# Sums across partitions: 56 small products a layer replaced by 32x32 turns and row sums, and one modulation group moved

## The chip, the core and the metric

The kernel runs on one core of one Trainium2 chip. The metric is the device time of one execution, in microseconds. Its engines work side by side and wait for each other through semaphores: TensorE (matrix products), VectorE (DVE), ScalarE (ACT), GpSimd (POOL), and SyncE (SP), whose queue here issues nearly all DMAs. An instruction is issued only when those before it in its own engine's program have been issued, so a wait holds everything behind it.

## The reference

Two layers of a decoder trunk, 1024 tokens of width 1024, all in f32. What matters here is the first half of a layer:

```python
mod = c_act @ ada_w[l] + ada_b[l]                      # six groups of 1024
sh1, sc1, g1, sh2, sc2, g2 = split(mod, 6)
h = rmsnorm(x, norm1_g[l]) * (1.0 + sc1) + sh1
proj = h @ w_in[l]                                     # in-projection, 20 column groups
y_ssd = ssd_mixer(...)                                 # conv, dt, chunked scan over 8 chunks of 128
y_mla = mla_mixer(...)                                 # rmsnorm(cq) @ w_uq, rmsnorm(ckv) @ w_ukv, attention
y_swa = swa_sink_mixer(...)
x = x + g1 * (concat(y_ssd, y_mla, y_swa) @ w_out[l])
h = rmsnorm(x, norm2_g[l]) * (1.0 + sc2) + sh2         # then the gated channel mixer, g2
```

Two kinds of sums across the partitions are touched: the sums over c of `c_act @ ada_w` for the groups g1, sh2, sc2, g2, and, per token, the sums of squares of the latents cq (256 channels) and ckv (128) for their RMS norms.

## The kernel before

A layer starts with the in-projection. The activations h lie with channels on partitions; the weight matrix is taken in 20 **packs** of 128 columns (pack 0: dt and the rotary key; 1 and 2: cq; 3: ckv; 4 to 11: the convolved channels; 12 to 15: the gate z; 16 to 19: the sliding-window heads). For each pack SyncE loads 512 KB into one of two `raw` tiles, ScalarE rounds it to a hi half (L984), GpSimd takes the lo half (L982), and TensorE does eight **K steps** of six 128x128x512 products (L1062): hi by hi, hi by lo, lo by hi, for two halves of the tokens. A pack's result stays in a bank pair (pack number mod 2) until ScalarE has copied it out, or, for packs 4 to 11, until VectorE has added three shifted taps of the convolution (L2216). Pack m waits for the release of pack m-2's bank (`pair_free`).

Between K steps TensorE is given other work by `scan_after`. In pack 7: the sums of squares of the latents. ScalarE has squared cq and ckv (L1774); `latent_sums` takes each 128x128 block as the stationary operand and one column of ones as the moving one, three products for each of eight blocks (L1143, L1144). In packs 10 and 11: the modulation sums. VectorE has multiplied 128 rows of `ada_w` at a time by `c_act` and added them up into an accumulator of 128x1024 for each of four groups (`early_products`, L2178 and L2181); `ada_half` sums its partitions with eight products of one column each (L1131). From pack 12 on: the **scan**, one chunk of 128 tokens in each pack's time. Its chain for chunk ch: ScalarE makes the decays from a tile that SyncE spreads over all partitions (`load_spread`, `cumSpread`, L790; `decays`, L1761 to L1766), VectorE multiplies the off-chunk part (`chunk_off`, L2287) and masks the scores (`mix`, L2252, L2254), TensorE does the diagonal products (`scan_back`, L1209).

The order on each engine is that of its program, written by hand. On VectorE: `early_products(0)` (eight passes), `dt_work` (a chain of passes of 8x1024 whose middle waits for ScalarE's Ln, and whose first part, `dt_sum`, that Ln waits for), then for j = 0 to 7 the taps of pack 4+j and, behind them, what the loop over j lists; then the scan. On ScalarE pack 1's eviction stands behind that Ln, and `decays(ch+1)` stands ahead of the hi half of pack 14+ch and of the eviction of pack 12+ch. On SyncE: ahead of pack 18's load stand eight loads of the latent up-projections (`wuq`, `wukv`), which go into the places of two modulation accumulators and so wait for `ada_part`; behind pack 18's load stands `load_spread(4)`, the fifth spread of decays.

Tiles share places. The weights `adaE` of groups 1 to 3 lie where x has been stored away; nt[2] and nt[3] are the accumulators of groups 0 and 1, and groups 2 and 3 accumulate in their own first tile. In layer 0 GpSimd also computes, in attention, the first two modulation groups of layer 1 (`ada_products`).

## Time and profile before

| | |
|---|---|
| median of 3 runs | 2359.29 us (2356.12 to 2361.5) |
| span of the profiled execution | 2356.7 us |
| TensorE busy | 2288.9 us, 97% of the span, 11493 products |
| VectorE busy | 1630.9 us, 69% |
| ScalarE, GpSimd busy | 1100.2 us, 1009.3 us |
| DMA | 310.98 MB, mean 132 GB/s |

The page gives the profiled execution's time by its span alone; the median of the runs is 2.6 us above it. "Busy" counts the time in which an engine works; TensorE's products are pipelined, so a group of rows can overlap the next by a few hundred ns. A wait in brackets behind a row is the idle time ahead of it and what ended it. The granted clock is TensorE's, 1.00 being the 2.4 GHz level and 0.50 the 1.2 GHz level.

### The profile page before, as it was taken

The page shows a single profiled execution, that of the slowest core. Times are in us where ns is not written, and L with a number is a line of the kernel's source. Part 1 is how long each engine was busy: PE and PEld are TensorE (multiplying, and loading weights), DVE is VectorE, ACT ScalarE, POOL GpSimd, SP SyncE. Part 2 cuts the span into 40 slices and gives each one's busy share as a digit, 9 for nine tenths or more (in the row PEclk, how much of TensorE's full clock was granted, in tenths as well). Part 3 has the DMA queues.
Part 4 walks back from the last instruction along what each step waited for, and adds up shares of the span by engine and source line. Part 5 has one row for each costly group of instructions (what it writes and reads, how often), then busy time and mean ns, then how long its engine had stood idle before and what let it go on. Part 6 is the DMA issues. An engine that isn't in the chain of part 4 may idle for free.

```text
span 2356.7 us, 31193 instructions
## 1 busy us (share of the span) xinstructions
PE 2288.9 (97%) x11493; PEld 1858.7 (79%) x11493; DVE 1630.9 (69%) x2084; ACT 1100.2 (47%) x1808; POOL 1009.3 (43%) x641
## 2 busy tenths in 40 slices
PE   5999999999899999999999999999999999999998
PEld 5788866788788888888878888668878888888887
DVE  6975457538876766777898644773697667677886
ACT  4335546524444444444452455673444444445455
POOL 1211268534987777400002123242479777760000
PEclk7999999999999999999999999999999999999999
DMA  8651323242333333487555331004414333347763
GB/s 287 221 196 54 77 63 117 99 139 85 92 112 90 112 90 117 144 293 252 156 194 191 108 85 55 10 20 153 142 41 125 112 90 112 90 130 254 246 214 112
DMA packets 272630, 310.98 MB, mean 132 GB/s; under 512 B 36905, under 2 KB 191263, under 8 KB 271455
## 3 DMA queue, kind: packets, MB, share of 16 engines
q1 hardware_dynamic: 272094, 307.94, 40.5%
q8 instruction: 92, 1.51, 0.3%
q10 hardware_dynamic: 384, 1.05, 0.2%
q14 instruction: 60, 0.48, 0.1%
HBM read 246.47 MB, written 61.42 MB: 131 GB/s over the span
## 4 chain that ended last, share of the span: by engine, by line
PE 80%; DVE 11%; ACT 2%; issue 2%; POOL 1%; DMA 1%; DVEq 0%; SPq 0%; ACTq 0%; POOLq 0%
PE bank L1489 30%; PE bank L1504 17%; PE bank L1062 16%; PE bank L1122 5%; DVE nt L2181 2%; PE bank L1320 2%; PE bank L1352 1%; PE bank L1280 1%; DVE hLo L2135 1%; PE bank L1380 1%; DVE xT L2129 1%; DMA raw<-in_ffn_w_up_dram 1%; PE bank L1209 1%; PE bank L1131 1%; DVE nt L2113 1%
## 5 line engine op out<-in xcount | busy, mean ns | idle before, releaser
L982 POOL TENSOR_TENSOR wLo<-raw,wHi 128x1024 fp32r<-128x1024 f32 x66 | 162.9, 2469 | 438.2 <-ACT wHi L984 438.2
L1681 POOL TENSOR_TENSOR prodLo<-comb,prodHi 128x512 fp32r<-128x512 f32 x160 | 234.3, 1471 | 123.6 <-ACT prodHi L1024 123.6
L1489 PE MATMUL bank<-tHi,prodHi 128*128 128x512 f32 x640 | 250.5, 391 | 5.2 <-DVE tLo L2493 4.1
L1489 PE MATMUL bank<-tLo,prodHi 128*128 128x512 f32 x640 | 249.9, 390 | 0.0
L1489 PE MATMUL bank<-tHi,prodLo 128*128 128x512 f32 x640 | 249.8, 390 | 0.0
L1504 PE MATMUL bank<-gateHi,downHi 128*128 128x512 f32 x616 | 240.5, 390 | 0.0
L1504 PE MATMUL bank<-gateHi,downLo 128*128 128x512 f32 x616 | 239.9, 389 | 0.0
L1504 PE MATMUL bank<-gateLo,downHi 128*128 128x512 f32 x616 | 239.8, 389 | 0.0
L1024 ACT ACTIVATE prodHi<-comb 128x512 fp32r<-128x512 f32 x160 | 100.5, 632 | 249.4 <-PE bank L1489 229.6
L2438 DVE SCALAR_TENSOR_TENSOR ub<-bank,ffp,ub 128x1023 f32<-128x1023 f32 x88 | 112.8, 1282 | 141.8 <-ACT ub L1943 140.2
L1062 PE MATMUL bank<-hHi,wHi 128*128 128x512 f32 x576 | 188.1, 408 | 5.4 <-ACT cq L1813 4.4
L1489 PE MATMUL bank<-hHi,prodHi 128*128 128x512 f32 x480 | 187.2, 390 | 6.2 <-POOL prodLo L1681 3.6
L1489 PE MATMUL bank<-hHi,prodLo 128*128 128x512 f32 x480 | 186.9, 389 | 0.0
L1489 PE MATMUL bank<-hLo,prodHi 128*128 128x512 f32 x480 | 186.8, 389 | 0.0
L984 ACT ACTIVATE wHi<-raw 128x1024 fp32r<-128x1024 f32 x66 | 69.5, 1055 | 239.9 <-PE bank L1062 166.2
L1062 PE MATMUL bank<-hLo,wHi 128*128 128x512 f32 x576 | 178.9, 392 | 0.0
L1062 PE MATMUL bank<-hHi,wLo 128*128 128x512 f32 x576 | 178.0, 390 | 0.0
L1681 POOL TENSOR_TENSOR prodLo<-raw,prodHi 128x512 fp32r<-128x512 f32 x120 | 165.2, 1404 | 0.0
L1489 PEld LDWEIGHTS bank<-tHi,prodHi 128*128 128x128 f32 x640 | 120.5, 188 | 32.4 <-DVE tLo L2493 5.0
L1489 PEld LDWEIGHTS bank<-tHi,prodLo 128*128 128x128 f32 x640 | 120.6, 188 | 25.1
L1489 PEld LDWEIGHTS bank<-tLo,prodHi 128*128 128x128 f32 x640 | 120.5, 188 | 24.8
L1504 PEld LDWEIGHTS bank<-gateHi,downHi 128*128 128x128 f32 x616 | 115.7, 188 | 24.3 <-issue 0.8
(392 smaller groups left out, 5401.4 us busy)
## 6 DMA issues: line engine op xcount, KB each, us to landing
raw<-in_ffn_w_up_dram SPq DMA_DIRECT2D x88, 512.0 KB, 5.2
gateRaw<-gateOut SPq DMA_DIRECT2D x154, 256.0 KB, 4.2
adaE<-in_ada_w_dram SPq DMA_DIRECT2D x64, 512.0 KB, 6.0
gateOut<-gateSums SPq DMA_DIRECT2D x22, 1024.0 KB, 5.4
raw<-in_w_in_dram SPq DMA_DIRECT2D x34, 512.0 KB, 4.4
downRaw<-in_ffn_w_down_dram SPq DMA_DIRECT2D x66, 256.0 KB, 3.6
raw<-in_w_out_dram SPq DMA_DIRECT2D x28, 512.0 KB, 4.2
downCols<-in_ffn_w_down_dram SPq DMA_DIRECT2D x24, 512.0 KB, 3.7
```

The lines of the kernel that those rows point to most:

```text
L982: eng.tensor_tensor(lo[:], raw[slot][:], fview(hi[:]), ALU.subtract).then_inc(s["split_lo"], 1)
L984: eng.activation((early_hi if n in (N_OUT0, N_PRE + 2) else third_hi if n == 2 else wHi[slot])[:], raw[slot][:], ACT.Copy).then_inc(s["spl ...
L1024: act.activation(sHiW[idx][:], product_source(js, idx), ACT.Copy).then_inc(s["us_hi"], 1)
L1062: last = mm(half(pair, hf), w(k), r(k)[:, HALF * hf:HALF * (hf + 1)], start=first and q == 0, stop=last_k and q == 2)
L1122: last = mm(o, w[n % 2][:, k * P:(k + 1) * P], r(k)[:, cols], start=first and q == 0, stop=last_k and q == 2)
L1131: last = mm(to[:, m:m + 1], acc[:, m * P:(m + 1) * P], caus01[:, P - 1:P], start=True, stop=True)
L1320: last = mm(bank[u % 2][:, q * HALF + a:q * HALF + b], qh[h][0:96, i * BLK:n], kh[h][0:96, a:b], start=True, stop=True)
L1489: last = mm(o, w[idx][:, c0], moving(idx, kp, hi), start=kp == 0 and q_ == 0, stop=kp == 3 and q_ == 2)
L1504: last = mm(down_bank(p, m), w[ring(n)][:, m * P:(m + 1) * P], g[ring(n)][:], start=i == 0 and q == 0, stop=i == NK - 1 and q == 2)
L1681: pool.tensor_tensor(sLoW[idx][:], product_source(js, idx), fview(sHiW[idx][:]), ALU.subtract).then_inc(s["us_lo"], 1)
L2181: ins = dve.scalar_tensor_tensor(out=acc[:], in0=adaE[j][k][:], scalar=cact[:, k:k + 1], in1=acc[:], op0=ALU.mult, op1=ALU.add)
L2438: dve.scalar_tensor_tensor(out=y[:, d:T], in0=bank[2 * q + b][:, 0:T - d], scalar=ffp[:, col:col + 1], in1=y[:, d:T], op0=ALU.mult, op1=AL ...
```

## The change

For the two kinds of sums the small products go. In their place VectorE **folds** a tile of 128x1024: it turns it in squares of 32x32 (`STREAM_TRANSPOSE`), after which the 32 partitions of a square lie along a row, and sums each run of 32 in a row (`TENSOR_REDUCE`): 128x32 remain. The four bands of 32 partitions are then brought together by four products with a fixed 0/1 matrix (`quad`): one set for the latents (after step 5 of pack 7), one for all four modulation groups (`mod_sums`, ahead of attention's first transposes). cq's two tiles of squares are first added on VectorE, so the latents need one add and two folds.

VectorE's program is reordered: `dt_work` is cut in two, with four of the eight products of group 0 ahead of its first part and four behind; group 1's products come six behind the first taps and two behind the second; group 2's behind the fourth and fifth; group 3's first four behind the seventh, its last four in the scan, two behind chunk 1 and two behind chunk 2; the fold of group 3 stands behind chunk 3. The weights of group 3 are loaded later. `mod` and `scl` are computed in attention's first unit instead of before the scan. SyncE's wait ahead of the up-projections is for four groups instead of two, and GpSimd's `ada_products` wait for the second set of small products.

```diff
@@ SyncE
                     if j >= 2:
-                        sp.wait_ge(s["ada_early"], nth("ada_early", KT * (j - 1) + k + 1))
+                        sp.wait_ge(s["ada_early"], nth("ada_early", KT * j + k - 3 if (j == 3 and k >= 4) else KT * (j - 1) + k + 1))
...
                 if kind == "win" and m == N_WIN - 2:
 
-                    sp.wait_ge(s["ada_part"], nth("ada_part", 2))
+                    sp.wait_ge(s["ada_part"], nth("ada_part", 4))
                     for k in range(2):
...
-                if kind == "win" and 9 <= m <= 12:
-                    if m == 11:
-                        sp.wait_ge(s["mn_sum"], nth("mn_sum", 1))
-                    load_early(2 + (m - 9) // 2, range(4 * ((m - 9) % 2), 4 * ((m - 9) % 2) + 4), m - 7)
+                if kind == "win" and m in (9, 10, 12, 14):
+                    g = (9, 10, 12, 14).index(m)
+                    load_early(2 + g // 2, range(4 * (g % 2), 4 * (g % 2) + 4), g + 2)
@@ TensorE
-            def ada_half(n):
-
-                ada_sum(n // 2, range(4 * (n % 2), 4 * (n % 2) + 4))
-
-            def latent_sums(b):
-
-                pe.wait_ge(s["mn_sq"], nth("mn_sq", 3))
-                for k in range(2):
-                    mm(half(2, 0)[:, b:b + 1], mnq[k][:, b * P:(b + 1) * P], ones, start=k == 0, stop=k == 1)
-                last = mm(half(2, 0)[:, NB + b:NB + b + 1], mnq[2][:, b * P:(b + 1) * P], ones, start=True, stop=True)
-                if b == NB - 1:
-                    last.then_inc(s["mn_sum"], 1)
+            def mod_sums():
+
+                pe.wait_ge(s["ada_part"], nth("ada_part", 4))
+                for r in range(4):
+                    last = mm(half(2, 1)[32 * r:32 * r + 32, 384:384 + 4 * KT], quad[:],
+                              foldA[:].rearrange("p j c -> p (j c)")[:, r:4 * 32:4], start=True, stop=True)
+                last.then_inc(s["ada_part"], 1)
+
+            def latent_sums(_):
+
+                pe.wait_ge(s["mn_sq"], nth("mn_sq", 6))
+                for r in range(4):
+                    last = mm(half(2, 0)[32 * r:32 * r + 32, 0:2 * NB], quad[:],
+                              foldL[:].rearrange("p j c -> p (j c)")[:, r:2 * 32:4], start=True, stop=True)
+                last.then_inc(s["mn_sum"], 1)
...
                 if m == 7:
-                    return {k: [(latent_sums, k)] if k < 6 else [(latent_sums, 6), (latent_sums, 7)] for k in range(KT - 1)}
+                    return {5: [(latent_sums, 0)]}
                 if m == 10:
-                    return {k: [(ada_half, k - 1)] + ([(chunk_ends, 0)] if k == 3 else []) for k in range(1, 7)}
+                    return {3: [(chunk_ends, 0)]}
                 if ch == -1:
-                    return {0: [(ada_half, 6)], 1: [(ada_half, 7)], 4: [(scan_turn, 0)]}
+                    return {4: [(scan_turn, 0)]}
...
+                if u == 0:
+                    mod_sums()
@@ GpSimd
                 pool.wait_ge(s["mn_sum"], nth("mn_sum", 1))
+                pool.wait_ge(s["ada_part"], nth("ada_part", 5))
@@ VectorE
                 dve.tensor_scalar(n2, n1, 1.0, None, ALU.add).then_inc(s["dt_sum"], 1)
+                yield
                 dve.wait_ge(s["dt_ln"], nth("dt_ln", 1))
...
+            def fold(src, to, sem, turned=foldT):
+
+                link(dve.transpose(turned[:], src))
+                dve.tensor_reduce(to, turned[:].rearrange("p (c i) -> p c i", i=32), AX.X, ALU.add).then_inc(s[sem], 1)
+
+            def mod_fold(j):
+
+                dve.wait_ge(s["ada_early"], nth("ada_early", KT * (j + 1)))
+                if j:
+                    dve.wait_ge(s["ada_part"], nth("ada_part", j))
+                fold((nt[2], nt[3], nt[3], nt[2])[j][:], foldA[:, j, :], "ada_part", nt[3] if j == 3 else foldT)
+
+            def latent_fold():
+
+                dve.wait_ge(s["mn_sq"], nth("mn_sq", 3))
+                dve.tensor_tensor(mnq[0][:], mnq[0][:], mnq[1][:], ALU.add).then_inc(s["mn_sq"], 1)
+                dve.wait_ge(s["mn_sq"], nth("mn_sq", 4))
+                fold(mnq[0][:], foldL[:, 0, :], "mn_sq")
+                dve.wait_ge(s["mn_sq"], nth("mn_sq", 5))
+                fold(mnq[2][:], foldL[:, 1, :], "mn_sq")
...
-            early_products(0, range(KT), 0)
-            dt_work()
+            early_products(0, range(4), 0, KT)
+            dt = dt_work()
+            next(dt)
+            early_products(0, range(4, KT), 0, KT)
+            for _ in dt:
+                pass
+            mod_fold(0)
...
                 if j == 0:
-                    early_products(1, range(KT), 1)
-                elif 2 <= j < 6:
-                    early_products(1 + j // 2, range(4 * (j % 2), 4 * (j % 2) + 4), j)
+                    early_products(1, range(6), 1, KT)
+                if j == 1:
+                    early_products(1, range(6, KT), 1, KT)
+                    latent_fold()
+                if j == 2:
+                    mod_fold(1)
...
+                if 1 <= ch < 3:
+                    early_products(3, range(2 * ch + 2, 2 * ch + 4), 5, 4)
+                if ch == 3:
+                    mod_fold(3)
```

How the instructions stand now. First VectorE at the start of a layer, before: the products of modulation group 0 (nt_60 is their accumulator), then the dt work, whose second row here is the step that ScalarE's Ln waits for.

```order
L2181 SCALAR_TENSOR_TENSOR nt_60<-adaE_3_84,cact,nt_60 128x1024
L2181 SCALAR_TENSOR_TENSOR nt_60<-adaE_4_85,cact,nt_60 128x1024
L2181 SCALAR_TENSOR_TENSOR nt_60<-adaE_5_86,cact,nt_60 128x1024
L2181 SCALAR_TENSOR_TENSOR nt_60<-adaE_6_87,cact,nt_60 128x1024
L2181 SCALAR_TENSOR_TENSOR nt_60<-adaE_7_88,cact,nt_60 128x1024
L2149 TENSOR_SCALAR hp<-hp 8x1
L2151 TENSOR_SCALAR dtWork_158<-dtWork_157 8x1024
L2153 TENSOR_SCALAR dtWork_158<-dtWork_158 8x1024
```

The same place after.

```order
L2188 SCALAR_TENSOR_TENSOR nt_60<-adaE_3_84,cact,nt_60 128x1024
L2155 TENSOR_SCALAR hp<-hp 8x1
L2157 TENSOR_SCALAR dtWork_161<-dtWork_160 8x1024
L2188 SCALAR_TENSOR_TENSOR nt_60<-adaE_4_85,cact,nt_60 128x1024
L2188 SCALAR_TENSOR_TENSOR nt_60<-adaE_5_86,cact,nt_60 128x1024
L2188 SCALAR_TENSOR_TENSOR nt_60<-adaE_6_87,cact,nt_60 128x1024
L2188 SCALAR_TENSOR_TENSOR nt_60<-adaE_7_88,cact,nt_60 128x1024
L2160 TENSOR_SCALAR dtWork_161<-dtWork_161 8x1024
```

The step that the Ln waits for has moved ahead of the last four products.

VectorE in the scan after the change, from the masks of chunk 3 (Mt is the masked decay) to the first passes of chunk 4.

```order
L2288 TENSOR_TENSOR bank<-bank,caus_264 128x128
L2290 TENSOR_TENSOR Mt_144<-Mt_144,bank 128x512
L2288 TENSOR_TENSOR bank<-bank,caus_264 128x128
L2290 TENSOR_TENSOR Mt_145<-Mt_145,bank 128x512
L2194 STREAM_TRANSPOSE nt_61<-nt_60 128x1024
L2195 TENSOR_REDUCE foldMod<-nt_61 128x32
L2218 TENSOR_TENSOR xdt<-bank,adt 128x512
L2220 COPY Btok<-bank 128x256
```

Before, the row of xdt follows that of the second Mt directly. On SyncE the loads that wait for this fold stand, before and after alike, in this order (wuq, wukv: up-projections; raw_52: pack 18; cumSpread: the spread for chunk 4):

```order
L806 DMA wuq<-in_mla_w_uq_dram 128x4x96 [waits ada_part]
L807 DMA wuq<-in_mla_w_uq_dram 128x4x16
L808 DMA wuq<-in_mla_w_uq_dram 128x4x16
...
L811 DMA wukv<-in_mla_w_ukv_dram 128x4x64 x2
L436 DMA raw_52<-in_w_in_dram 128x8x64 [waits split_lo,split_hi]
L436 DMA raw_52<-in_w_in_dram 128x8x64
L791 DMA cumSpread<-cumOut 128x1024 [waits sd_eb,sd_seg]
```

Here no row has moved; what has moved is the place in VectorE's program of the fold that ends the first row's wait.

## Rows read from the trace of the kernel before

**Rows 1.** Part 4 of the page: shares of the chain by engine.

```profile
PE 80%; DVE 11%; ACT 2%; issue 2%; POOL 1%; DMA 1%; DVEq 0%; SPq 0%; ACTq 0%; POOLq 0%
```

**Rows 2.** Busy time by stretch: from:to, length, engines, granted clock, DMA.

```profile
134.60:149.90 15.30, 15.26 (x91) 13.52 (x92) 8.36 (x7) 2.78 (x3) 2.40 (x1) 1.00 0.19 59
196.80:326.20 129.40, 127.86 (x720) 105.67 (x720) 56.35 (x117) 66.60 (x118) 33.53 (x22) 1.00 0.25 68
```

**Rows 3.** Chain in order of time, pack 7: start us, us, what.

```profile
134.64 1.61 PE bank L1062 x6
...
136.82 1.49 PE bank L1062 x6
...
149.81 12.41 PE bank L1062 x54
```

**Rows 4.** Chain in order of time, pack 10: two groups of modulation sums.

```profile
178.43 0.79 PE bank L1131 x8
...
180.72 0.78 PE bank L1131 x8
```

**Rows 5.** Timelines of four engines, layer 0: start, us, engine, line [idle before].

```profile
74.25 13.25 DVE L2181 SCALAR_TENSOR_TENSOR nt<-adaE,cact,nt 128x1024 f32<-128x1024 f32 x7
...
81.21 2.56 POOL L982 TENSOR_TENSOR wLo<-raw,wHi 128x1024 fp32r<-128x1024 f32 x1 [4.75 <-ACT wHi L984]
...
88.30 1.06 ACT L1823 ACTIVATE dtWork<-dtWork 8x1024 f32<-8x1024 f32 x1 [5.86 <-DVE dtWork L2151]
...
90.40 0.70 PE L1062 MATMUL bank<-hHi,wHi 128*128 128x512 f32 x2 [2.02 <-ACT cq L1813]
```

**Rows 6.** Timeline of TensorE, layer 1, start of pack 3.

```profile
1238.08 0.70 PE L1062 MATMUL bank<-hHi,wHi 128*128 128x512 f32 x2 [2.42 <-ACT cq L1813]
```

**Rows 7.** Busy time by stretch, with the granted clock behind POOL's.

```profile
24.00:28.00 4.00, 0.00 (x0) 0.00 (x0) 3.69 (x4) 3.96 (x7) 0.00 (x0) 0.54 1.00 306
...
56.00:58.00 2.00, 2.00 (x5) 1.26 (x5) 1.97 (x3) 1.28 (x2) 0.00 (x0) 0.50 1.02 385
...
1240.00:1242.00 2.00, 2.00 (x6) 1.61 (x5) 2.00 (x1) 0.00 (x0) 1.94 (x1) 0.50 1.03 414
```

**Rows 8.** Timeline of VectorE: taps of pack 5; a row sum in attention.

```profile
130.59 3.91 DVE L2216 SCALAR_TENSOR_TENSOR xbc<-bank,prm,xbc 128x1023 f32<-128x1023 f32 x3
...
366.09 1.22 DVE L2324 TENSOR_REDUCE stat_s<-swaProb 128x4 f32<-128x1028 f32 x1
```

**Rows 9.** Line L2181: shortest, median and longest instruction in ns.

```profile
L2181 DVE SCALAR_TENSOR_TENSOR nt<-adaE,cact,nt x28: 1283/1285/3419, 74.2 to 1278.7; 128x1024 f32<-128x1024 f32 x28
```

**Rows 10.** Timeline of SyncE's queue in the scan: up-projections, pack 18, spread.

```profile
245.40 0.61 SPq L805 DMA_DIRECT2D wuq<-in_mla_w_uq_dram  x1
...
250.69 1.32 SPq L810 DMA_DIRECT2D wukv<-in_mla_w_ukv_dram  x2
259.83 1.01 SPq L432 DMA_DIRECT2D raw<-in_w_in_dram  x2
260.94 0.87 SPq L790 DMA_DIRECT2D cumSpread<-cumOut  x1
```

**Rows 11.** Timeline of VectorE, end of chunk 3 and chunk 4.

```profile
261.84 0.69 DVE L2254 TENSOR_TENSOR Mt<-Mt,bank 128x512 f32<-128x512 f32 x1
265.14 0.69 DVE L2190 TENSOR_TENSOR xdt<-bank,adt 128x512 f32<-128x512 f32 x1 [2.61 <-PE bank L1170]
...
275.60 0.30 DVE L2252 TENSOR_TENSOR bank<-bank,caus 128x128 f32<-128x128 f32 x1 [1.85 <-PE bank L1195]
```

**Rows 12.** Timelines of ScalarE, TensorE and GpSimd: chunk 4; start of `ada_products`.

```profile
266.10 1.28 ACT L1761 ACTIVATE Mt<-cumSpread,adt 128x128 f32<-128x128 f32 x4 [6.49 <-DMA cumSpread<-cumOut]
...
271.04 0.63 ACT L1764 ACTIVATE pairDecay<-cumSpread 64x512 f32<-64x512 f32 x1
...
278.22 1.09 PE L1209 MATMUL bank<-Mt,xdt 128*64 128x128 f32 x16
...
338.95 1.89 POOL L1591 TENSOR_TENSOR nt<-raw,cact 128x1024 f32<-128x1024 f32 x1
```

More of the change, by code:

```diff
@@ L273, in build @@
     yLo = place("ssdLo", [P, 4, T], F32R, E[8])
-    adaE = [[place(f"adaE{j}_{k}", [P, D], F32, E[8 + k] if j == 0 else at["f"] if (j, k) == (3, 0) else at["x"] + 4 * K * k)
+    adaE = [[place(f"adaE{j}_{k}", [P, D], F32, E[8 + k] if j == 0 else at["x"] + 4 * K * (k % 4 if j == 3 else k))
              for k in range(KT)] for j in range(4)]
+    foldT = place("foldTurned", [P, T], F32, E[3])
+    foldA = place("foldMod", [P, 4, 32], F32, at["f"] + 5 * K)
+    foldL = place("foldLatent", [P, 2, 32], F32, at["f"] + 5 * K + 512)
     R = [at["h"] + 4 * K * i for i in range(16)]
@@ L357, in build @@
     dshift = small("shiftStep", [P, 4])
+    quad = small("quadSum", [P, 32])
     bank = [nc.alloc_psum_tensor(f"bank{i}", [P, 1024], F32) for i in range(4)]
@@ L597, in _ @@
                 dve.wait_ge(s["ident_ready"], 4)
+                link(dve.tensor_reduce(quad[:], ident[:].rearrange("p (r j) -> p j r", r=4), AX.X, ALU.add))
                 link(dve.tensor_copy(nt[2][lo, :], posi[lo, :]))
@@ L1125, in ada_sum @@
             def ada_sum(j, ms=range(KT)):
-                pe.wait_ge(s["ada_early" if j < 4 else "ada_used"], nth("ada_early" if j < 4 else "ada_used", KT * (j + 1 if j < 4 else j - 3)))
-                acc = (nt[2], nt[3], adaE[2][0], adaE[3][0], nt[0], nt[1])[j]
-                to = ada_at(j) if j < 4 else half(2, 1)[:, 384:384 + KT]
+                pe.wait_ge(s["ada_used"], nth("ada_used", KT * (j - 3)))
+                acc = (nt[0], nt[1])[j - 4]
+                to = half(2, 1)[:, 384:384 + KT]
                 for m in ms:
@@ L2239, in _ @@
                     scan_turned(0)
+                    early_products(3, range(4), 4, 4)
                 if j == 7:
-                    dve.wait_ge(s["ada_part"], nth("ada_part", 4))
                     dve.memset(hst[0][:], 0.0).then_inc(s["sd_h"], 1)
-                    dve.tensor_tensor(mod[:, 2 * KT:6 * KT], half(3, 1)[:, 256:256 + 4 * KT], prm[:, R_ADAB + 2 * KT:R_ADAB + 6 * KT],
-                                      ALU.add).then_inc(s["mod_rest"], 1)
-                    dve.wait_ge(s["mod_rest"], nth("mod_rest", 1))
-                    link(dve.scalar_tensor_tensor(out=scl[:, 1, :], in0=mod[:, 4 * KT:5 * KT], scalar=1.0, in1=prm[:, R_N2:R_N2 + KT],
-                                                  op0=ALU.add, op1=ALU.mult))
             def mix(ch, g):
@@ L2358, in beside_probs @@
                 dve.wait_ge(s["un_t"], nth("un_t", u + 1))
+                if u == 0:
+                    dve.wait_ge(s["ada_part"], nth("ada_part", 5))
+                    dve.tensor_tensor(mod[:, 2 * KT:6 * KT], sums[:, 384:384 + 4 * KT], prm[:, R_ADAB + 2 * KT:R_ADAB + 6 * KT],
+                                      ALU.add).then_inc(s["mod_rest"], 1)
+                    dve.wait_ge(s["mod_rest"], nth("mod_rest", 1))
+                    link(dve.scalar_tensor_tensor(out=scl[:, 1, :], in0=mod[:, 4 * KT:5 * KT], scalar=1.0, in1=prm[:, R_N2:R_N2 + KT],
+                                                  op0=ALU.add, op1=ALU.mult))
                 if u == SUMS_AT[1]:
```

23 lines of the change are left out of this document (13 added, 10 removed), and 4 rows, old and new, of the table PER_LAYER.

## The prediction, as put on record before the run

> **What bounds the kernel now.** I read the page's chain of waits first. TensorE carries 80% of it and VectorE 11% [rows 1], so what is taken off TensorE counts only where TensorE is the last to be ready. Next the busy time by stage: from 134.6 us on, the in-projection and the scan of layer 0 keep TensorE busy without a break (15.26 of 15.3 us in pack 7, 127.86 of 129.4 us in the scan [rows 2]). A product taken out there shortens the kernel by its full step, until another engine is late. Layer 1 repeats the pattern 1149 us later. Then I followed, in order of time, the four engines and the DMA queue of SyncE around each place that the change touches. All times below are layer 0's unless said.
>
> **The change, part by part.**
>
> *Latent sums, removed (24 products in pack 7).* A K step of a pack is six matmuls and takes 10.88/8 = 1.36 us: packs 3 to 6 take 133.9 - 90.4 = 43.5 us. In pack 7 the steps start 2.05 to 2.18 us apart [rows 3]. The pack starts at 134.64; its last step starts at 149.81 [rows 3], so pack 8 starts at 151.2: 16.55 us where a bare pack takes 10.9. Removed: 5.65 us.
>
> *Modulation sums, removed (32 products in packs 10 and 11).* With a group of four the step is 2.29 us (group at 178.43, next at 180.72 [rows 4]) instead of 1.36: 0.93 a group, eight groups, 7.45 us. Both together 13.1 us a layer.
>
> *The dt work split around the first modulation products.* Now ScalarE's Ln waits until 88.3 for a VectorE step queued behind eight products (73.46 to 87.5), and the eviction that frees pack 3's bank stands behind the Ln [rows 5]. TensorE waits 2.02 us at pack 3 in layer 0 [rows 5] and 2.42 in layer 1 [rows 6]. With only four products ahead, the step ends near 81, the Ln at 83.5, the eviction at 84.4, before pack 2 ends at 88.2. The whole wait goes: 2.15 us. In layer 1 the granted clock then fell to 0.50 (the 1.2 GHz level) for some 3.2 us after that wait [rows 7], so 1.6 us more: 4.0 there.
>
> *Six instead of eight products before the second convolution.* TensorE waits at pack 7 for the taps that end at 134.5 [rows 8]; bare packs would have ended at 133.9. With 2.6 us fewer ahead they end near 131.2, before pack 6 does (131.75). Gain 0.7 us a layer. Late next: the third convolution.
>
> *Folds, added on VectorE.* A fold is one transpose of 128x1024 and one row sum. A row sum of 128x1028 took 1.22 us [rows 8]; no transpose stands in the trace. From below 0.69, a VectorE pass over half as many elements [rows 11]; from above 3.42, the dearest pass of this size, a product beside GpSimd's split [rows 9]. I take 1.22, nearest to a pass that reads one tensor once: 2.45 a fold. By the Trainium skill ("Vector Engine (DVE) Microarchitecture Reference", section 3.8) a 32x32 turn sustains one element per cycle per lane, which with that page's slope makes about 1.14 us, an estimate; no run so far shows it. Fold 0 follows dt work: 111.4 to 113.9, while the first convolution waits for ScalarE until about 112.5; nothing waits for that 1.4 us. The latent work is different. After the second convolution (131.2) come two products (2.6), an add (1.2) and two folds (4.9): 140.1, or 142.1 if the add or a product meets GpSimd's split, as the products beside the split at 81.21 did: seven lasted 13.25 us [rows 5] where the median is 1.285 [rows 9], two stretched by 2.0 each. TensorE wants the folds after step 5 of pack 7, at 139.9; then four products and two steps; and behind the folds stands the third convolution, which frees pack 8's bank at 144.0 to 146.0. Pack 8 starts at 145.1 on the middle value, against 142.65 for a bare pack: cost 2.45 us a layer. On contention the row shows a stretched pass with two SBUF inputs. The Trainium skill ("GPSIMD Engine Reference") names as contending only VectorE instructions with two SBUF inputs or in a 2-port mode; by that the folds stay at 2.45 beside a split, while folds held like the products would be 2.0 longer each, 4 us more in pack 7. The rows show neither for a transpose.
>
> *Four small products for latents, four for modulation.* Each lies under the 0.235 us that a removed one costs, above nothing: I take 0.15, so 0.6 a set. The first set is in the 145.1. The second stands ahead of attention's first transposes, where TensorE itself waits (1.4 us) for ScalarE; it comes behind that wait in program order, so 0.6 us a layer is paid.
>
> *Modulation group 3 moved into the scan.* Its products fill holes: 2.6 us behind the second chunk's masks, where VectorE idles 2.61 us in every chunk [rows 11]; the same behind the third. Its fold stands behind chunk 3's masks, which end at 262.5 [rows 11], so it ends at 265.0. VectorE is free until 265.14 [rows 11]. **But SyncE's queue waits for this fold.** Ahead of pack 18's load it waits for all four groups (before: two), then issues eight loads of the latent up-projections, pack 18's two and the fifth decay spread. Today the eight go out from 245.40 to 252.01, in the shadow, and the spread at 260.94 [rows 10]. Moved, the eight begin at 265.05 and take 6.6 us, pack 18's 1.1, and the spread goes out at 272.8: 11.8 us later. ScalarE's decays of chunk 4 start when it lands, 266.10 today [rows 12], 277.9 then. The pair decay's second half ends 5.6 us after the start [rows 12], then come the off-chunk product (a 128x512 pass, 0.7) and the masks (twice 0.30 and 0.69, 2.0) [rows 11], so the diagonal products can start at 286.1. Today they start at 278.22 [rows 12]. TensorE stands for 7.9 us; in layer 1 the same sum gives 7.4, since its spreads land sooner. Queued behind the decays on ScalarE are the hi half of pack 17 and pack 15's eviction: 287.3 with GpSimd's half, before TensorE is through the end of pack 16 (289.1), so no more wait there. The next spread waits for that split and lands at about 293.4, hidden or 0.7 us.
>
> *Clock.* While TensorE stood still in the prologue the granted clock fell to 0.54 of full, and after 2.4 us in layer 1 to 0.50 [rows 7]. Half rate lasted 3.2 us of work in layer 1, and about 6 us from 52.3, where work restarts, to past 58 [rows 7]: 1.6 to 3 us lost. I add 2.3 a layer: 10.2 and 9.7 us.
>
> *GpSimd in layer 0.* The next layer's products started at 338.95 [rows 12]; now they wait for the new sums near attention's start, some 11 us later against TensorE. The chain later waits for a load that attention's progress releases, which takes up most of it, but more of it runs beside attention's VectorE passes: 0.5 us.
>
> **Sum.** Layer 0: -13.1 - 2.15 - 0.7 + 2.45 + 10.2 + 0.6 + 0.5 = -2.2. Layer 1: -13.1 - 4.0 - 0.7 + 2.45 + 9.7 + 0.6 = -5.05. Together -7.25 on the profiled execution's 2356.7 us. The median of the runs is 2.6 us above it; I carry that over: 2359.3 - 7.3 = 2352.
>
> **Rivals.**
> A (60%): as above; own range 2346 to 2360, from the clock (3 us), contention in pack 7 (4 us for both layers) and where the small products fall.
> B (17%), the queue wait costs nothing or little: SyncE issues the eight loads faster with nothing else in flight, or the decays have room. Against it: eight issues took 6.6 and 6.4 us in the two layers, and ScalarE already waits for this very spread. Without the 19.9 us the time is 2332.
> C (15%), slower: the turn itself is slow. Each us above 1.22 counts twice in pack 7 and once in the scan, 3 a layer, 6 in all. From 2.4 us a turn on, the kernel is slower than before; at the 3.42 bound it adds 13.2: 2365. For it: no row shows the instruction. Against: it reads and writes each element once.
> D (8%), no gain to spend: the third convolution or the folds eat twice what I allow, or the half clock comes in pack 7 too (2.4 us waits did that once); about 2358.
>
> **Numbers.** 0.2%, about 4.7 us, is what a measurement of this kernel can tell from none. A lies below 2354.6 in two of three cases, above 2364 in 3 of 100, else within; B is faster, D within, C slower. Faster 0.57, same 0.26, slower 0.17. The range 2334 to 2362 leaves out half of B and most of C.
>
> **What would show it.** Steps of pack 7 at 1.36 us, no wait at pack 3, clock 1.00 through layer 1's packs 3 and 4. Pack 12 starting 12 to 15 us earlier. SyncE's eight loads directly behind the fold of group 3, the decays of chunk 4 waiting for their spread some 12 us longer, and one TensorE wait of 7 to 8 us at the diagonal products of chunk 4 in each layer, with a clock of 0.50 behind it. If that wait is under 3 us, A is wrong and B right; if a transpose lasts over 2.4 us, C. Wrong in another way would be waits in chunks 1 to 3, where group 3's last loads now stand ahead of pack 14's and the second spread.

## The result, and the profile after

| | time, us | range | ratio to before |
|---|---|---|---|
| kernel before, 20 runs | 2357.02 | 2354.97 to 2361.99 | |
| changed kernel, 20 runs | 2362.05 | 2358.64 to 2364.95 | 1.0016 [1.0009, 1.0022] |

I forecast 2352, faster. It is slower: by 5.0 us between the medians, by 3.8 us or 0.16% between the means, which the ratio compares. That is about the 0.2% that I called the limit of measurement, but with 20 runs on each side the interval excludes no change. The profiled execution of the changed kernel is the shortest of its 20, 3.4 us under their median, and has the same span as that of before, 2356.9 against 2356.7 us. What makes up the 3.4 is the last experiment below.

The page of the kernel after, its totals and the chain [rows 1]:

```profile
PE 2268.6 (96%) x11301; PEld 1836.4 (78%) x11301; DVE 1674.7 (71%) x2111; ACT 1100.9 (47%) x1808; POOL 1014.7 (43%) x641
...
PE 75%; DVE 15%; issue 3%; ACT 2%; DMA 1%; POOL 1%; SPq 1%; DVEq 0%; ACTq 0%; POOLq 0%
```

TensorE is busy 20.3 us less (2288.9 before): the products are gone. Its share of the chain fell from 80 to 75% and VectorE's rose from 11 to 15%. The 20 us were not lost in the new products; somebody else became last.

Pack 7, and a stretch as long as the second of [rows 2] that begins as far ahead of the scan; the columns are the same:

```profile
134.50:148.70 14.20, 11.60 (x56) 9.00 (x56) 13.96 (x11) 1.82 (x3) 1.68 (x1) 1.00 0.41 134
187.40:316.80 129.40, 120.87 (x665) 100.15 (x664) 65.69 (x117) 67.11 (x117) 33.73 (x22) 0.97 0.30 84
```

In pack 7 VectorE is busy 13.96 of 14.2 us and TensorE 11.6, where TensorE had been busy 15.26 of 15.3. In the scan TensorE stands still 8.5 us instead of 1.5, and the granted clock is 0.97.

TensorE's timeline, layer 0, packs 6, 7 and 8 (start, us, engine, line, and in brackets the idle time before it and who ended it):

```profile
121.40 0.47 PE L1062 MATMUL bank<-hHi,wHi 128*128 128x512 f32 x1 [1.28 <-DVE xbc L2249]
...
134.51 0.47 PE L1062 MATMUL bank<-hHi,wHi 128*128 128x512 f32 x1 [1.96 <-DVE xbc L2249]
...
144.84 0.25 PE L1147 MATMUL bank<-foldLatent,quadSum 128*32 128x16 f32 x6 [1.92 <-DVE foldLatent L2195]
...
148.75 0.47 PE L1062 MATMUL bank<-hHi,wHi 128*128 128x512 f32 x1 [0.72 <-DVE xbc L2249]
```

Four waits for VectorE, 5.88 us, where before there were two waits, 2.48 us (2.02 at pack 3, for ScalarE [rows 5], and 0.46 at pack 7). The wait at pack 3 is gone, as forecast. In layer 1 the first two of the four are absent in this execution; pack 8 starts there at 1298.12.

VectorE's timeline in the same stretch, and GpSimd's splits beside it:

```profile
89.00 3.29 DVE L2162 TENSOR_TENSOR dtWork<-dtWork,dtWork 8x1024 f32<-8x1024 f32 x1
...
100.14 3.31 DVE L2165 TENSOR_TENSOR dtWork<-dtWork,dtWork 8x1024 f32<-8x1024 f32 x1
...
117.35 1.27 DVE L2249 SCALAR_TENSOR_TENSOR xbc<-bank,prm,xbc 128x1023 f32<-128x1023 f32 x1
...
134.28 2.98 DVE L2188 SCALAR_TENSOR_TENSOR nt<-adaE,cact,nt 128x1024 f32<-128x1024 f32 x1
...
139.75 1.25 DVE L2194 STREAM_TRANSPOSE foldTurned<-latentSq 128x1024 f32<-128x1024 f32 x1
141.03 1.22 DVE L2195 TENSOR_REDUCE foldLatent<-foldTurned 128x32 f32<-128x1024 f32 x1
...
144.70 1.27 DVE L2249 SCALAR_TENSOR_TENSOR xbc<-bank,prm,xbc 128x1023 f32<-128x1023 f32 x1
```

```profile
88.72 2.50 POOL L982 TENSOR_TENSOR wLo<-raw,wHi 128x1024 fp32r<-128x1024 f32 x1 [4.79 <-ACT wHi L984]
99.60 2.78 POOL L982 TENSOR_TENSOR wLo<-raw,wHi 128x1024 fp32r<-128x1024 f32 x1 [8.38 <-ACT wHi L984]
110.48 2.40 POOL L982 TENSOR_TENSOR wLo<-raw,wHi 128x1024 fp32r<-128x1024 f32 x1 [8.10 <-ACT wHi L984]
```

The transpose lasts 1.25 us and the row sum 1.22: a fold costs what I took. But fold 0 ends at 117.4, not 113.9, so the first convolution starts at 117.35, and the third at 144.70, not 140 to 142. VectorE has no gap from 72.97 to 148.6; three passes of the dt work are stretched (the two above by 2.1 us each; the eight scans behind 110.21, beside the third split, last 4.83 us where they took 2.62), where before one was, by 2.0.

The queue of SyncE in chunks 3 and 4, and what waited for it on ScalarE and TensorE ([rows 10] and [rows 12] are the same places before, some 9.4 us later on the clock):

```profile
255.56 0.61 SPq L806 DMA_DIRECT2D wuq<-in_mla_w_uq_dram  x1
...
259.58 1.30 SPq L811 DMA_DIRECT2D wukv<-in_mla_w_ukv_dram  x2
260.98 1.19 SPq L436 DMA_DIRECT2D raw<-in_w_in_dram  x2
262.27 0.79 SPq L791 DMA_DIRECT2D cumSpread<-cumOut  x1
...
267.68 1.28 ACT L1765 ACTIVATE Mt<-cumSpread,adt 128x128 f32<-128x128 f32 x4 [17.38 <-DMA cumSpread<-cumOut]
...
275.93 0.48 PE L1210 MATMUL bank<-Mt,xdt 128*64 128x128 f32 x2 [7.05 <-DVE Mt L2290]
```

Here the forecast holds almost to the row: eight loads behind the fold of group 3, the spread 6.7 us behind the first of them, ScalarE idle 17.38 us instead of 6.49, one TensorE wait of 7.05 us (7.22 in layer 1; forecast 7.9 and 7.4).

Clock behind that wait, and at the start of attention in layer 0 (stretch, length, busy times, granted clock, DMA):

```profile
276.00:280.00 4.00, 4.00 (x24) 3.51 (x25) 0.58 (x1) 1.16 (x2) 1.27 (x1) 0.50 0.42 89
...
352.00:358.00 6.00, 5.68 (x28) 3.99 (x30) 3.46 (x9) 2.48 (x10) 5.88 (x3) 0.51 0.42 114
```

The first was forecast, the second not. Timelines of attention's start, layer 0:

```profile
349.46 0.30 PE L1139 MATMUL bank<-foldMod,quadSum 128*32 128x32 f32 x8 [1.38 <-ACT prob L1868]
...
352.32 0.44 PE L1355 MATMUL bank<-ident,prob 128*128 128x128 f32 x1 [1.32 <-DVE probT L735]
...
349.93 1.89 POOL L1595 TENSOR_TENSOR nt<-raw,cact 128x1024 f32<-128x1024 f32 x1 [11.09 <-issue]
...
350.40 1.45 DVE L2404 SCALAR_TENSOR_TENSOR scl<-mod,prm 128x8 f32<-128x8 f32 x1
351.88 0.29 DVE L735 COPY probT<-bank 128x128 f32<-128x128 f32 x1
```

The pass for the second scale, of 8 elements, took 1.45 us beside GpSimd's first product (0.17 in layer 1, where GpSimd has none). The copy that TensorE waits for stands behind it, so a second wait of 1.32 us follows the 1.38, and then TensorE runs six us at the lower clock.

Landmarks of the two traces give each term (us; minus is a gain):

| stretch | layer 0: forecast | measured | layer 1: forecast | measured |
|---|---|---|---|---|
| end of pack 2 to pack 7 | -2.85 | 0.93 | | |
| pack 7 | -3.2 | -2.3 | | |
| both | -6.05 | -1.4 | -7.9 | -7.15 |
| packs 8 to 11 | -7.45 | -6.95 | -7.45 | -7.0 |
| scan, up-projections | 10.2 | 9.2 | 9.7 | 9.75 |
| attention | 1.1 | 3.8 | 0.6 | 0.45 |
| sum | -2.2 | 4.7 | -5.05 | -3.95 |

For instance, layer 0's first row: pack 2 ends at 88.38 and pack 7 starts at 134.64 before, 87.32 and 134.51 after. The rest of the span differs by less than 1.3 us at any one place (the start is 1.06 shorter, since the clock came back sooner from the prologue). Layer 1's -7.15 is that of a short execution: in the second profile of the changed kernel, the last experiment below, the same stretch gives -3.2.

### The profile page after: what moved, and what is told of

It reads as the page before. It is cut to its first block, busy times and chain, and to the rows that moved or that the text cites. A ratio compares the mean times of both kernels' runs of the same rounds, so it can differ in the third digit from the quotient of the medians.

```text
span 2356.9 us, 30850 instructions
## 1 busy us (share of the span) xinstructions
PE 2268.6 (96%) x11301; PEld 1836.4 (78%) x11301; DVE 1674.7 (71%) x2111; ACT 1100.9 (47%) x1808; POOL 1014.7 (43%) x641
## 4 chain that ended last, share of the span: by engine, by line
PE 75%; DVE 15%; issue 3%; ACT 2%; DMA 1%; POOL 1%; SPq 1%; DVEq 0%; ACTq 0%; POOLq 0%
PE bank L1492 30%; PE bank L1507 17%; PE bank L1062 12%; PE bank L1122 5%; DVE nt L2188 2%; PE bank L1321 2%; PE bank L1355 1%; PE bank L1281 1%; DVE hLo L2141 1%; PE bank L1383 1%; DVE xbc L2249 1%; DMA raw<-in_ffn_w_up_dram 1%; DVE xT L2135 1%; PE bank L1210 1%; DVE nt L2119 1%
```

## The experiments

All ratios are of means, to executions of the kernel before that were measured beside it, with 95% intervals. A difference to the changed kernel is one of medians that were not measured side by side; from the ratios the first three and the split undone come out as 17.2, 4.0, 0.9 and 5.4 us.

**The loads behind the spread.** SyncE's block is moved, nothing else:

```diff
-                if kind == "win" and m == N_WIN - 2:
-                    sp.wait_ge(s["ada_part"], nth("ada_part", 4))
-                    ... (the eight loads)
                 if n >= AHEAD:
                     load_pack(n, kind, m)
                 if SCAN0 + 3 <= n < N_WIN:
                     load_spread(n - SCAN0 - 2)
+                if kind == "win" and m == N_WIN - 2:
+                    sp.wait_ge(s["ada_part"], nth("ada_part", 4))
+                    ... (the eight loads)
```

> The changed kernel with one edit: SyncE's wait for the last modulation fold and the eight loads of the latent up-projections stand behind pack 18's load and the fifth decay spread instead of ahead of them. Theory (the queue behind that wait made the stall): the TensorE waits of 7.05 and 7.22 us at the diagonal products of chunk 4 go, and with them the stretches at half clock (about 2.1 us a layer), so attention of layer 0 starts some 9 us earlier than in the changed kernel (349.5) and the kernel takes 18 us less than it: 2339 to 2345, ratio to the kernel before 0.993 to 0.995. Rival (the decays of chunk 4 are late for another reason, or the loads in their new place hold up the next spread or arrive too late for the up-projections): a wait of over 3 us stays in the scan or appears at the up-projections near 317 us, and the gain is under 10 us.

2344.86 us, 0.9943 [0.9931, 0.9955]: 17 us less than the changed kernel. SyncE and ScalarE in that kernel:

```profile
250.62 0.81 SPq L791 DMA_DIRECT2D cumSpread<-cumOut  x1
...
255.58 1.28 ACT L1765 ACTIVATE Mt<-cumSpread,adt 128x128 f32<-128x128 f32 x4 [6.28 <-DMA cumSpread<-cumOut]
```

ScalarE waits 6.28 us, as it did before the change, and no wait of chunk 4 is left. Attention of layer 0 starts at 339.31 instead of 349.46. The queue theory is shown: the stall goes with the order of the queue. By itself this edit turns the change from a loss into a gain of 13 us.

**Fold 0 later.**

```diff
             for _ in dt:
                 pass
-            mod_fold(0)
 ...
                 if j == 2:
+                    mod_fold(0)
                     mod_fold(1)
```

> The changed kernel with one edit: the fold of modulation group 0 (transpose and row sum, 2.45 us on VectorE) stands behind the third convolution, next to that of group 1, instead of ahead of the first. Theory (VectorE's queue from 74 to 148 us is what sets the start of pack 8): every us taken out of it ahead of the third convolution is a us less of TensorE waits (1.28 at 121, 1.96 at 134.5, 1.92 ahead of the small products, 0.72 at pack 8), so pack 8 starts 2.0 to 2.5 us earlier than 148.75, in both layers, and the kernel takes 4 to 5 us less than the changed one: near 2357, ratio to the kernel before 0.999 to 1.001. Rival (TensorE's waits there come from ScalarE's evictions or from contention with GpSimd wherever the passes stand): pack 8 moves by under 1 us and the time stays at 2362.

2356.85 us, 0.9999 [0.9991, 1.0008]: 5.2 us less than the changed kernel. TensorE's waits from 74 to 150 us, and the clock behind the longer one:

```profile
PE bank L1147 <- DVE foldLatent L2195: 2.2, 1, 2.2
PE bank L1062 <- DVE xbc L2248: 1.0, 1, 1.0
```

```profile
144.00:146.00 2.00, 2.00 (x6) 1.52 (x6) 1.93 (x2) 0.00 (x0) 0.00 (x0) 0.50 0.00 0
```

The waits fell from 5.88 to 3.16 us in layer 0, but the one of 2.2 brought the lower clock, which took some of it back: attention starts only 0.4 us earlier there, with pack 3 0.9 later. In layer 1 none of the four waits is left and attention starts 3.9 us earlier. So VectorE's queue did set pack 8; but pack 8 starts 0.6 us earlier in layer 0 and 4.3 in layer 1, so the forecast for each layer (2.0 to 2.5) fits only on the mean.

**GpSimd's products one unit later** (layer 0's attention):

```diff
-                pool.wait_ge(s["ada_part"], nth("ada_part", 5))
+                pool.wait_ge(s["un_cd"], nth("un_cd", 1))
```

> The changed kernel with one edit: GpSimd's products for the next layer (layer 0 only) wait until VectorE has copied the first unit's transposes in attention, about 1 us later than now. Theory (the small pass that makes the second scale was held 1.45 us instead of 0.17 by GpSimd's first product, the copy behind it made TensorE wait 1.32 us right after a wait of 1.38, and the granted clock then stood at 0.50 for some 6 us): the pass takes 0.2 us, the second wait goes, the clock stays at 1.00, and layer 0's out-projection starts about 3 us earlier (459 instead of 462.1); layer 1 is unchanged. The kernel takes 2 to 4 us less than the changed one: 2358 to 2360, ratio to before 1.000 to 1.001. Rival (layer 0's attention is late because GpSimd's whole chain is 11 us later): the out-projection starts at 462 or later and the time does not fall.

2360.84 us, 1.0012 [1.0003, 1.0021]. The small pass and TensorE's next wait:

```profile
349.71 0.17 DVE L2404 SCALAR_TENSOR_TENSOR scl<-mod,prm 128x8 f32<-128x8 f32 x1
...
352.83 0.41 PE L1355 MATMUL bank<-ident,prob 128*128 128x128 f32 x2 [0.84 <-ACT probT L735]
```

The mechanism is shown: 0.17 us, the wait of 1.32 gone, the clock 1.00 from 349 to 360, and layer 0's out-projection starts at 458.25 instead of 462.07, 3.8 us earlier where I expected 3. But the medians differ by 1.2 us only. Against the first profile of the changed kernel the gain is gone by pack 8 of layer 1 (1297.95 against 1298.12), because VectorE's stretch up to the third convolution lasted 71.7 us instead of 67.95. That is no cost of this edit, though: the second profile of the changed kernel has 71.8 us there too and starts that pack at 1302.01, so against it all of the gain is still there. This profiled execution is also 2.45 us under its own median. Why the medians show a third of the 3.8 us stays open.

**The split alone**, on the kernel before (the dt work's first step behind four products instead of eight; the cut in `dt_work` and the wait for all eight weight loads at the first products, which go with it, are left out here):

```diff
-            early_products(0, range(KT), 0)
-            dt_work()
+            early_products(0, range(4), 0)
+            dt = dt_work()
+            next(dt)
+            early_products(0, range(4, KT), 0)
+            for _ in dt:
+                pass
```

> The kernel before with one part of the change: the dt work's first step stands behind four modulation products instead of eight, everything else as before. Theory (as predicted for this part): the waits at pack 3 (2.02 and 2.42 us) and layer 1's stretch at half clock go, and TensorE keeps what it gains: 2.2 us in layer 0, 4 in layer 1, so 2350 to 2352, ratio to before 0.997 to 0.998. Rival (VectorE is the last to be ready at packs 5 to 7, so TensorE only waits later): waits of 1 to 2 us appear at packs 5 to 7, the gain is under 3 us, ratio 0.999 to 1.000.

2363.65 us, 1.0035 [1.0023, 1.0047]: slower by 6 us. Both theories were too kind. TensorE at pack 7, and the clock behind it:

```profile
133.92 0.77 PE L1062 MATMUL bank<-hHi,wHi 128*128 128x512 f32 x1 [3.74 <-DVE xbc L2221]
```

```profile
134.00:156.00 22.00, 22.00 (x68) 18.55 (x68) 8.04 (x7) 0.86 (x1) 0.00 (x0) 0.50 0.14 45
```

The 2.02 us of pack 3 came back in the 3.74 at pack 7, and then TensorE ran at the 1.2 GHz level from 133 to about 157 us: pack 8 starts at 161.01, 9.9 us later than before. Not all of the 3.74 is the edit's: in this execution pack 2 ended 1.9 us earlier than in the profile of before. But all six executions took 2362.6 us or more. In layer 1, where VectorE had had 3.6 us to spare at the first convolution, the wait at pack 7 is 0.45 as before and the layer gained 4.3 us, near the 4 forecast.

**The split undone in the changed kernel** (all eight products ahead of the dt work again).

> The changed kernel with one part undone: the dt work behind all eight products of group 0. Theory (VectorE's queue sets pack 8, so a wait of TensorE at pack 3 is covered by the 5.9 us it waits later anyway, and the split saves only VectorE's own wait of 1.12 us for the logarithm): 0 to 2.5 us more than the changed kernel, 2362 to 2365, ratio to before 1.001 to 1.003, by pieces of 2.1 either way where one more or less of VectorE's passes meets GpSimd's split. Rival (the split is worth 2.15 and 4.0 us, as predicted): 2368, ratio 1.0045.

2356.16 us, 0.9993 [0.9984, 1.0002]: 5.9 us less than the changed kernel, where I expected more time by either theory. GpSimd and VectorE in layer 0:

```profile
101.97 3.08 POOL L982 TENSOR_TENSOR wLo<-raw,wHi 128x1024 fp32r<-128x1024 f32 x1 [8.48 <-ACT wHi L984]
...
102.82 2.77 DVE L2168 TENSOR_SCALAR dtWork<-misc,hp 8x1024 f32<-8x1024 f32 x1
...
139.66 1.27 DVE L2247 SCALAR_TENSOR_TENSOR xbc<-bank,prm,xbc 128x1023 f32<-128x1023 f32 x1
```

The third convolution starts at 139.66, 5 us earlier. The wait of 2.11 us at pack 3 is TensorE's only one up to pack 8. The splits follow TensorE's packs; held by that wait, they stand beside other passes of the dt work (at 90.47 instead of 88.72, while a pass already runs and then beside the reciprocal of 6.54 us, neither stretched; at 101.97 instead of 99.60), and one dt pass is stretched instead of three.

**The latent part alone**, on the kernel before (its products replaced by the folds and four small products, all else as before).

> The kernel before with one part of the change: the latent sums by folds on VectorE behind the second convolution and four small products after step 5 of pack 7; the modulation sums, the dt work and SyncE's order stay as in the kernel before. Theory (in the changed kernel it is fold 0 and the late dt work that make VectorE late at pack 7, not the latent folds): in layer 0 the second convolution ends at 134.5, as in the kernel before, add and folds at 140.6, which is before TensorE is through step 5 (142.9), the third convolution at 144.5, before pack 8's bank is wanted (145.7): no wait, 5.4 us less a layer, 2346 to 2348, ratio to before 0.995 to 0.996. Rival (the latent folds are themselves the cost, by contention with GpSimd's split or through the third convolution): waits of 1.5 us or more ahead of the small products or at pack 8, gain under 3 us a layer, ratio 0.9975 or more.

2349.71 us, 0.9964 [0.9951, 0.9978]: 8 us less, where I expected 11 (the interval reaches from 5 to 11.6) and the rival under 6. VectorE's third convolution, and TensorE at pack 7 and at the first wait of the scan:

```profile
142.76 1.27 DVE L2234 SCALAR_TENSOR_TENSOR xbc<-bank,prm,xbc 128x1023 f32<-128x1023 f32 x1
```

```profile
136.79 0.47 PE L1067 MATMUL bank<-hHi,wHi 128*128 128x512 f32 x1 [0.45 <-DVE xbc L2234]
...
207.48 0.48 PE L1191 MATMUL bank<-xdtEnd,Btok 128*128 128x256 f32 x1 [0.61 <-POOL xdtEnd L1617]
```

No wait stands at the small products or at pack 8. From pack 7 (before 134.64) to that wait in the scan (before 210.40) layer 0 is 5.1 us shorter, and layer 1 5.0: the folds are hidden and the products' time is gained. The other 2 us lie elsewhere: the lower clock came behind the wait at pack 3 of layer 0 instead of layer 1, which nearly cancels out, and 2.1 are lost in layer 1's attention, where it came once (1504 to 1507); whether they belong to the edit stays open.

**Four edits together:** the loads, fold 0, GpSimd's products, and the last two products of group 1 behind the latent folds:

```diff
                 if j == 1:
-                    early_products(1, range(6, KT), 1, KT)
                     latent_fold()
+                    early_products(1, range(6, KT), 1, KT)
```

> The changed kernel with four edits at once: the up-projection loads behind the fifth spread, the fold of group 0 behind the third convolution, the last two products of group 1 behind the latent folds instead of ahead of them, and GpSimd's products of layer 0 held until the first unit's copy. Theory (the four waits are separate, and with VectorE no longer last at pack 8 what attention gains in layer 0 isn't given back in layer 1): 12 us from the loads, as measured, 5 from the fold, as measured, 2 to 4 from the two products (the latent folds end 2.6 to 4.3 us earlier, and 2.2 us of wait stood before the small products), 3 to 5 from attention: 2331 to 2337, ratio to the kernel before 0.989 to 0.9915. Rival (VectorE's queue up to the third convolution is still last, or the third convolution is now late behind the folds): no more than the loads and the fold bring, 2340 to 2342, ratio 0.993.

2333.2 us, 0.9892 [0.9879, 0.9906]: 25 us less than the kernel before, as expected. TensorE's waits for the convolutions from 74 to 330 us:

```profile
PE bank L1062 <- DVE xbc L2248: 2.1, 2, 1.1
```

A split of GpSimd and a transpose that lies wholly beside it:

```profile
131.81 3.13 POOL L982 TENSOR_TENSOR wLo<-raw,wHi 128x1024 fp32r<-128x1024 f32 x1 [5.19 <-ACT wHi L984]
...
132.69 1.25 DVE L2194 STREAM_TRANSPOSE foldTurned<-latentSq 128x1024 f32<-128x1024 f32 x1
```

**The same without the split.**

> The kernel with the four edits, but the dt work again behind all eight products of group 0, as in the kernel before. Theory (with VectorE's queue lightened TensorE is last at packs 3 to 7, so the split is now worth what I predicted for it): waits of 2.0 and 2.4 us are back at pack 3, layer 1 with half clock behind it, and the kernel takes 3 to 6 us more than with the split. Rival (VectorE's queue still ends last at pack 7, as it did with the split alone, where the wait of 2.0 at pack 3 came back as 3.74 at pack 7): within 2 us of the version with the split.

2337.51 us, 0.9914 [0.9899, 0.9929]: 4.3 us more than with the split, though with four and five executions the two intervals overlap. TensorE at pack 3, layer 0, and the clock:

```profile
90.02 0.47 PE L1062 MATMUL bank<-hHi,wHi 128*128 128x512 f32 x1 [2.40 <-ACT cq L1819]
```

```profile
90.00:94.00 4.00, 3.98 (x11) 3.12 (x12) 3.93 (x3) 1.73 (x2) 2.98 (x1) 0.59 1.02 406
```

The profiles bear the sign out: from the start of pack 2 to pack 8 both layers take 68.2 us with the split and 70.0 without. So one and the same edit costs 5.9 us in the changed kernel, where TensorE's waits for VectorE in pack 7 are 1.96 and 1.92 us, and is worth some 4 here, where those at packs 7 and 8 are down to 1.10 and 0.95.

**Group 1 thinned**: four products behind the first convolution, four behind the third.

```diff
                 if j == 0:
-                    early_products(1, range(6), 1, KT)
+                    early_products(1, range(4), 1, KT)
 ...
                 if j == 2:
+                    early_products(1, range(4, KT), 1, KT)
                     mod_fold(0)
```

> The version with four edits, and one more: of group 1's eight products only four stand behind the first convolution (before: six), the other four behind the third, ahead of the folds of groups 0 and 1. Theory (VectorE's queue is still last at packs 7 and 8 there: waits of 1.10 and 0.95 us in each layer): 2.6 us less of VectorE before the second convolution and 2.6 less before the third remove both waits, 2.0 us a layer, 4 in all: 2328 to 2331, ratio to before 0.987 to 0.989. Rival (the passes only move to where something else waits for them: GpSimd's splits now meet other two-input passes, or the fourth convolution comes late): a wait of 1 us or more at packs 7 to 10 and the time of the version with four edits, 2333, or more.

2344.77 us, 0.9946 [0.9934, 0.9959]: 11.6 us more than with four edits. The theory's first half came true: no wait is left at packs 7 and 8, and pack 8 starts at 142.12 instead of 144.21. But the rival was right, and by both things that it named. VectorE and TensorE:

```profile
140.36 7.27 DVE L2188 SCALAR_TENSOR_TENSOR nt<-adaE,cact,nt 128x1024 f32<-128x1024 f32 x4
...
152.55 3.91 DVE L2248 SCALAR_TENSOR_TENSOR xbc<-bank,prm,xbc 128x1023 f32<-128x1023 f32 x3
156.38 0.24 DVE L2253 RECIPROCAL rst<-rst 128x16 f32<-128x16 f32 x1
...
156.68 0.54 PE L449 MATMUL bank<-ident,rst 128*128 128x128 f32 x3 [3.52 <-DVE rst L2253]
```

The four products take 2.1 us more than four undisturbed ones, because GpSimd's split at 143.51 falls among them. VectorE has no gap from 136.53 on, the fourth convolution starts at 152.55 (149.00 with four edits), and TensorE waits 3.52 us for the reciprocal behind it. A wait of 2.51 us for GpSimd follows in the scan (201.33), and behind both the granted clock falls to the lower level. SyncE's queue was late too: group 2's weights go into the buffers that the delayed products read, so they were issued one by one, and ScalarE waited 6.83 us for the weights of the next pack behind them. But its hi half was done at 155.1 and the reciprocal at 156.6, so in this profile VectorE was the one that ended TensorE's wait.

**The changed kernel once more.**

> The changed kernel, unedited, one more look. Its profiled run was the shortest of 20 (2358.64 against a median of 2362.05), and in it VectorE's stretch from the first product of group 0 to the third convolution lasted 67.95 us in layer 1, where layer 0's, and layer 1's in two edited versions, lasted 71.7, with one or two more passes stretched beside GpSimd's split. Theory: that stretch in layer 1 is what differs from run to run, so a run near the median has 71.7 us there, TensorE waits of 1.28 and 1.96 us at the packs before and the third at 1298 or later, and is 2 to 4 us longer. Rival: layer 1's stretch is 67.95 again whatever the time, and the difference lies elsewhere (the start, layer 0's attention).

2362.45 us (one run, before 2357.55 beside it). Layer 1, VectorE and TensorE:

```profile
1242.14 3.47 DVE L2162 TENSOR_TENSOR dtWork<-dtWork,dtWork 8x1024 f32<-8x1024 f32 x1
```

```profile
1274.67 0.70 PE L1062 MATMUL bank<-hHi,wHi 128*128 128x512 f32 x2 [1.41 <-DVE xbc L2249]
...
1287.78 0.47 PE L1062 MATMUL bank<-hHi,wHi 128*128 128x512 f32 x1 [1.96 <-DVE xbc L2249]
```

VectorE starts group 0 at 1226.12 in both executions, but the third convolution starts at 1297.96 instead of 1294.07: the dt pass that took 1.21 us takes 3.47, others changed with it, and both waits that the first profile lacked are there. What decides it is who begins first, by less than 0.1 us. That pass begins at 1242.14 in both; GpSimd's split, in the first profile and then in the second:

```profile
1242.21 3.41 POOL L982 TENSOR_TENSOR wLo<-raw,wHi 128x1024 fp32r<-128x1024 f32 x1 [5.14 <-ACT wHi L984]
...
1242.13 2.41 POOL L982 TENSOR_TENSOR wLo<-raw,wHi 128x1024 fp32r<-128x1024 f32 x1 [5.06 <-ACT wHi L984]
```

In the first the pass ran through and the split lasted 1 us longer; in the second the split ran through and the pass ended 1.08 us behind it. Span 2360.7, 3.8 more. So layer 1's 71.8 us, and not 67.95, is what this execution near the median has, and that difference of 3.9 us covers the 3.4.

## Why the prediction was wrong, step by step

**Where it failed.** "The whole wait goes: 2.15 us" and "With 2.6 us fewer ahead they end near 131.2, before pack 6 does", with "Fold 0 follows dt work: 111.4 to 113.9 ... nothing waits for that 1.4 us". Three terms that I booked apart all rest on when VectorE is through its queue at packs 5 to 8, and I moved TensorE's end of that race without moving GpSimd's splits with it. The wait at pack 3 did go. But VectorE has the second convolution ready at 134.3 with or without it, so TensorE stood later; and the earlier splits met two more dt passes. The dt work ended at 115.0 instead of 111.4. Measured: +0.93 instead of -2.85 for packs 3 to 6 in layer 0. The split alone and the split undone show it from both sides, and fold 0 moved shows that the 2.45 us which I called free were paid, 4 to 5 us in both layers together. In layer 1 the same step failed less visibly: -7.15 instead of -7.9 in the first profile, -3.2 in the second, which is nearer to the median.

**Pack 7:** the two folds, add and products took what I said, 10.4 us with one product stretched by 1.7, but started 3.1 us late. The gain was 2.3 instead of 3.2. On the kernel before, where they start in time, the latent folds are free: here my 2.45 a layer was too much.

**Products removed:** in packs 8 to 11 -6.95 and -7.0 for -7.45. Right.

**The queue of SyncE:** wait, loads, spread, decays, stall and clock came as written, 9.2 and 9.75 us for 10.2 and 9.7. Shown by moving the loads. The largest single loss of the change was right.

**Attention:** layer 1 0.45 for 0.6. Layer 0 3.8 for 1.1: I had counted GpSimd's later start as more contention, 0.5 us, and had not asked what a pass of 0.17 us does to the copy behind it when GpSimd starts at that moment, nor that a second wait close behind one of 1.38 can bring the lower clock. The held products show the mechanism, 3.8 us at the out-projection; that the medians show only 1.2 us of it stays open.

**Rivals.** B (the queue wait costs little) is excluded. C (slow transposes) too: 1.21 to 1.25 us in all 12. D came nearest, "the third convolution or the folds eat twice what I allow", 2358, though the cause was the start of the folds. I gave it 8%. The bound that the range lacked is the stretch: I let it hit only the latent folds, 4 us, and not the dt work. On contention, the transpose at 132.69 in the version with four edits lay wholly beside a split and took 1.25 us, and so did a row sum of the changed kernel (149.79, split from 149.26 to 151.67: 1.22). That agrees with the Trainium skill ("GPSIMD Engine Reference", section "Key points"), by which the folds stay at 2.45 us. The 1.14 us, an estimate, that the Trainium skill ("Vector Engine (DVE) Microarchitecture Reference", section 3.8) led to for the turn is 0.1 short of the trace.

## What to carry to other kernels

When a wait is taken away on one engine, lay the other engines' queues beside the new schedule up to the next place where they meet. The wait is gained only if each of them has more slack there; an edit can cost 6 us in one version and bring some 4 in the next, so judge it again after the bound has moved. Before adding a wait to a queue that issues in order, list every load behind it; often the block can stand two instructions later for nothing, which here was worth 17 us.

## What the runs showed of the hardware

- How long TensorE waits does not alone decide whether its clock falls. At packs 3 to 8 waits of 1.9 to 2.1 us mostly left the granted clock at 1.00 (2.02, 2.11, 1.96, 1.92), but one of 1.98 in layer 1 of the kernel with the loads moved brought 0.50 until about 1283. One of 2.21 and five of 2.40 or 2.42 brought 0.50 for some 3 to 4 us; a sixth, of 2.42 in layer 1 of the kernel with the latent part alone, did not. Nor does the wait decide how long the lower level lasts: some 5 us after 7 us, 3 to 7 after 1.38 and 1.32 close together, 3 to 4 after 3.52 (group 1 thinned, layer 0), 24 after 3.74. In the four edits without the split a wait of 1.38 alone, at 338.0, had 0.50 behind it for 3 to 4 us. What decides stays open.
- VectorE and GpSimd keep each other out in some passes, and whichever begins first runs through. A two-input VectorE pass of 1.21 to 1.29 us that begins while a split runs ends 1.07 to 1.09 us behind the split, and so lasts 2.93 to 3.47 us; a split that begins while such a pass runs ends 2.2 to 2.4 us behind the pass, and so lasts up to 1.2 us longer than its 2.4. Where a split had itself been held by a TENSOR_SCALAR, the two-input pass behind that one ran through as well, 14 times, and the split lasted 3.6 us. A TENSOR_SCALAR and a COPY with one input were held too (0.74 and 0.68 to 2.77), and a pass of 0.17 us beside GpSimd's product (1.45). Transposes, row sums, the reciprocal and passes that read a bank were never held in the twelve traces.
- Two executions of one program took 67.95 and 71.84 us for the same stretch of VectorE, because a split began 0.07 us behind a pass in one and 0.01 us ahead of it in the other, and others changed with it. Terms near such a boundary belong in the range.
